# Latent attention of the prompt with its keys in the partitions, and a join without it

## Reference

```python
k_nope = einsum('bsc,chd->bshd', c_kv, w_uk);  v = einsum('bsc,chd->bshd', c_kv, w_uv)
s = (einsum(q_nope, k_nope) + einsum(q_pe, k_pe)) * MLA_SCALE    # 64 + 32 rows; MLA_SCALE = 96 ** -0.5
s = where(kpos <= qpos, s, -inf);  p = softmax(s);  ob = einsum('bhqk,bkhd->bqhd', p, v)
oa = merge of three dilated window attentions, weighted by their softmax denominators
pa = (oa * silu(za)) @ w_proj_a;   pb = (ob * silu(zb)) @ w_proj_b
```

## Time and profile before

| | |
|---|---|
| median of 3 runs | 4224.75 us (4222.05 to 4228.91) |
| the profiled execution | 4216.9 us, its span 4215.3 us |
| PE, DVE, ACT, POOL busy in it | 3469.0, 1314.7, 957.4, 281.4 us |
| latent attention, from 2385 to 3147 us of the span | 762 us |
| join, from 3617 to 3787 us | 170 us |

### The profile page before, as it was taken

How to read it: one execution, slowest core, us unless ns; L and a number is a source line. 1 busy time by engine, 2 the same in 40 slices (tenths; PEclk the granted TensorE clock), 3 DMA queues, 4 the chain that set the end, 5 groups by cost and what they waited for, 6 DMA issues and landing times. The chain is left out here.

```text
span 4215.3 us, 55290 instructions
## 1 busy us (share of the span) xinstructions
PE 3469.0 (82%) x19384; PEld 2980.1 (71%) x19384; DVE 1314.7 (31%) x3532; ACT 957.4 (23%) x1846; POOL 281.4 (7%) x308
## 2 busy tenths in 40 slices
PE   3899999999988897999999799999982444318989
PEld 3777777877776686999999677777762444318877
DVE  4122211222222122221111255555541222583333
ACT  4322211222211112222222144444430000001021
POOL 0000000000000000000000000000001222003300
PEclk6999999999978887999999899999995555559999
DMA  3233333333122223322222200000005554565443
GB/s 109 63 101 107 108 105 111 113 105 105 57 80 80 88 75 89 94 84 80 78 86 77 66 12 12 12 12 12 12 17 190 187 188 150 185 213 202 153 135 117
DMA packets 349533, 407.90 MB, mean 97 GB/s; under 512 B 113066, under 2 KB 306315, under 8 KB 347099
## 3 DMA queue, kind: packets, MB, share of 16 engines
q1 hardware_dynamic: 328330, 258.31, 20.7%
q0 software_dynamic: 21008, 147.09, 9.6%
HBM read 318.18 MB, written 175.19 MB: 117 GB/s over the span
## 5 line engine op out<-in xcount | busy, mean ns | idle before, releaser
L109 PE MATMUL dil_S<-all_xT_hi,dil_w_hi 128*128 128x512 f32 x1152 | 467.7, 406 | 17.6 <-DVE dil_w_lo L621 17.6
L110 PE MATMUL dil_S<-all_xT_lo,dil_w_hi 128*128 128x512 f32 x1152 | 461.2, 400 | 0.0
L111 PE MATMUL dil_S<-all_xT_hi,dil_w_lo 128*128 128x512 f32 x1152 | 460.3, 400 | 0.0
L109 PE MATMUL gate_ps<-all_xT_hi,gate_w_hi 128*128 128x416 f32 x960 | 346.4, 361 | 13.7 <-DVE gate_w_lo L1074 13.7
L111 PE MATMUL gate_ps<-all_xT_hi,gate_w_lo 128*128 128x416 f32 x960 | 338.1, 352 | 0.0
L110 PE MATMUL gate_ps<-all_xT_lo,gate_w_hi 128*128 128x416 f32 x960 | 337.4, 351 | 0.0
L1525 PE MATMUL mla_S<-mla_k,mla_q 96*128 96x512 f32 (+3 forms) x640 | 276.7, 549 | 15.2 <-ACT mla_p L1416 9.2
L109 PEld LDWEIGHTS dil_S<-all_xT_hi,dil_w_hi 128*128 128x128 f32 x1152 | 222.0, 193 | 67.3 <-DVE dil_w_lo L621 17.8
L1553 PE MATMUL mla_O<-mla_v,mla_pT 128*128 128x66 f32 x2176 | 264.3, 271 | 2.6 <-DVE mla_pT L1474 1.7
L1553 PEld LDWEIGHTS mla_O<-mla_v,mla_pT 128*128 128x128 f32 x2176 | 257.6, 192 | 5.0 <-DVE mla_pT L1474 2.6
L111 PEld LDWEIGHTS dil_S<-all_xT_hi,dil_w_lo 128*128 128x128 f32 x1152 | 220.5, 191 | 51.5
(11 more groups left out here) (263 smaller groups left out, 5790.0 us busy)
## 6 DMA issues: line engine op xcount, KB each, us to landing
out_win_sample<-in_state_win POOLq DMA_DIRECT2D x16, 4088.0 KB, 14.8
sdil_kv<-in_state_win SPq DMA_DIRECT2D x72, 512.0 KB
scr_gates<-gate_out POOLq DMA_DIRECT2D x120, 208.0 KB, 2.2
sdil_qb<-scr_hs SPq DMA_DIRECT2D x32, 768.0 KB
dil_raw<-in_w_in SPq DMA_DIRECT2D x36, 512.0 KB, 4.1
proj_gm<-scr_gates SPq DMA_DIRECT2D x40, 416.0 KB, 3.3
gate_ckv<-in_cache_ckv SPq DMA_DIRECT2D x256, 64.0 KB, 1.8
out_win_sample<-in_state_win POOLq DMA_DIRECT2D x4, 4064.0 KB, 2.3
```

Source lines behind the costliest of these rows:

```text
L109: pe.matmul(out, w[0], x[0], start=first, stop=False)
L110: pe.matmul(out, w[0], x[1], start=False, stop=False)
L111: return pe.matmul(out, w[1], x[0], start=False, stop=last)
```

## Change

The latent attention is written anew. A unit is now one head with 512 queries (`qb`, 4 of them); its tiles are 128 keys in the partitions by 512 queries, `4 * qb + 4` of them, of which the last four lie on the diagonal and have 512, 384, 256 and 128 queries. That is 40 tiles and 17,408 columns a head. The values of all heads are projected once, ahead (16 products of 512 columns). Queries and keys are split into high and low parts. A tile goes: scores by `split_matmul` (item A), copy to SBUF by ACT into one of 22 slots `sc`, on the diagonal the mask by DVE, running maximum over the unit's tiles by DVE; the unit's maxima are turned by PE (M1), reduced and widened by DVE, turned again (M2) and copied by ACT into `mb`, one maximum for each query in all partitions; POOL subtracts `mb` from each tile in SBUF, ACT takes the exponential in place, and PE multiplies values (64 columns beside 64 columns of ones) with the tile, so that outputs and sums come out turned (item B). DVE inverts 64x512 sums, POOL multiplies with the gates, DVE multiplies with the output, and SP stores 64x512 straight into `scr_uT`. The order of all this is a list that `latent_order` makes ahead of time. The join keeps only the dilated part.

```diff
 def stage_latent_attn(nc, t, ident):
-        RING = 6
-        S = m.ps("S", [P, 4, 512])
-        T = m.ps("T", [P, 2, 4, P])
+        RING = 22
+        LAG = 12
+        LEAD = 4
+        tiles, first, order = latent_order(RING, LAG)
+        sc = m.sb("sc", [P, RING, 512])
+        PJ = m.ps("PJ", [P, 512])
+        S = m.ps("S", [P, 2, 512])
+        T = m.ps("T", [P, 4, P])
...
+        def values_due(p, lead, begun):
+            i = begun
+            while i < NTILES and place[("B", i)] <= p + lead and place[("M2", unit(i))] <= p:
+                i += 1
+            return range(begun, i)
...
+                    sp.dma_start(causal[:, :], t["causal"].rearrange("a b -> b a")).then_inc(loaded, 16)
...
             def _(pool):
+                def weigh(n, begun):
+                    r = out_rows(n // 4)
+                    pool.wait_ge(centred, begun)
+                    pool.wait_ge(inverted, n + 1)
+                    pool.wait_ge(gz_in[n % 2], 16 * (n // 2 + 1))
...
+                    pool.tensor_tensor(rg[r, :], rv[r, :], gz[n % 2][r, :], ALU.mult).then_inc(rg_ready, 1)
...
+                    for i in values_due(p, LEAD + 3, begun):
+                        x = sc[:, i % RING, c0:512]
+                        pool.wait_ge(mb_out, n + 1)
+                        pool.tensor_tensor(x, x, mb[n % 2][:, c0:512], ALU.subtract).then_inc(centred, 1)
...
+                        act.wait_ge(s_ready, i + 1)
...
+                        act.activation(sc[:, i % RING, c0:512], S[:, i % 2, c0:512], ACT.Copy).then_inc(copied, 1)
...
+                    for i in values_due(p, LEAD, begun):
+                        act.wait_ge(centred, i + 1)
+                        act.activation(x, x, ACT.Exp, scale=B_SCALE).then_inc(exped, 1)
...
+                        dve.tensor_tensor(top[:, c0:512], old[:, c0:512], new[:, c0:512], ALU.max).then_inc(maxed, 1)
...
+                        dve.reciprocal(rv[out_rows(n // 4), :], O[s, n % 2, :]).then_inc(inverted, 1)
...
+                pe.wait_ge(loaded, 16 * 7)
...
+                        split_matmul(pe, S[:, i % 2, c0:512], [k[x][0:W, kt * P:(kt + 1) * P] for x in range(2)],
+                                     [q[x][0:W, qb * 512 + c0:(qb + 1) * 512] for x in range(2)], True, True)\
+                            .then_inc(s_ready, 1)
...
+                        pe.matmul(O[:, n % 2, c0:512], w, sc[:, i % RING, c0:512], start=kt == 0,
+                                  stop=kt == 4 * qb + 3).then_inc(pv_ready, 1)
 def stage_join(nc, t, ident, wraw):
-                    sp.dma_start(ob[b][:, 0:chunks, :, :], t["ob"][rows, 0:chunks]).then_inc(oin[b], 16)
...
-                    sp.dma_start(gz[b][:, :, :], t["gates"][0:8, :, rows].rearrange("k p n -> p k n"))\
+                    sp.dma_start(gz[b][:, :, :], t["gates"][0:4, :, rows].rearrange("k p n -> p k n"))\
...
+def latent_order(ring, lag):
...
+        if can_value() and (not can_go() or (not took_value and scored - valued > lag)):
+            order.append(("B", valued))
+            now += max((512 - tiles[valued][3]) * 0.00168, 0.23)
...
+        elif can_go():
+            item = ahead.pop(0)
+            order.append(item)
+            if item[0] == "A":
+                h, qb, kt, c0 = tiles[item[1]]
+                now += max((512 - c0) * 0.00133, 0.33)
```

More of the change, by code:

```diff
@@ new lines, in _ @@
+                for c in range(QL // P):
+                    sp.dma_start(cqT[:, c, :], t["cqT"][c, :, 0:SEQ]).then_inc(loaded, 16)
+                sp.dma_start(kpe[NOPE:W, :], t["kpeT"][:, 0:SEQ]).then_inc(loaded, 16)
+                sp.dma_start(rope[NOPE:P, :], t["rope_cols"][:, 0:SEQ]).then_inc(loaded, 16)
+                with nc.allow_non_contiguous_dma(reason="the mask, turned"):
+                    sp.dma_start(causal[:, :], t["causal"].rearrange("a b -> b a")).then_inc(loaded, 16)
@@ new lines, in _ @@
+                load_weights(1)
+                for n in range(4 * H):
+                    h, qb, b = n // 4, n % 4, n % 2
+                    if n > 1:
+                        sp.wait_ge(rg_ready, n - 1)
+                    r = out_rows(h)
+                    sp.dma_start(gz[b][r, :], t["gates"][4 + h // 2, r, qb * 512:(qb + 1) * 512]).then_inc(gz_in[b], 16)
+                    if n:
+                        store(n - 1)
+                    if qb == 2 and h < H - 2:
+                        load_weights(h + 2)
@@ L1432, in _ @@
-                each_head(act, body)
+                r, pe = slice(0, NOPE), slice(NOPE, W)
+                act.wait_ge(loaded, 16 * 7)
+                act.activation(k[0][pe, :], kpe[pe, :], ACT.Copy).then_inc(kpe_hi, 1)
+                for j in range(0, NT, 2):
+                    act.wait_ge(v_ready, j + 1)
+                    act.activation(v[:, j, :, 0:3:2, :], S[:, 0, :].rearrange("p (a s d) -> p a s d", s=2, d=HD), ACT.Copy)\
+                        .then_inc(v_out_a, 1)
+                begun = 0
@@ new lines, in body @@
+                    maxima = [rec[:, g, :, 2 * HD + 2:REC] for g in range(NG)]
+                    w3 = [heads(wt[:, g * H:(g + 1) * H]) for g in range(NG)]
+                    s3 = [heads(sl[:, g * H:(g + 1) * H]) for g in range(NG)]
+                    top = heads(mx[:, :])
+                    then(dve.tensor_tensor(top, maxima[0], maxima[1], ALU.max))
+                    then(dve.tensor_tensor(top, top, maxima[2], ALU.max))
+                    for g in range(NG):
+                        last = dve.tensor_tensor(w3[g], maxima[g], top, ALU.subtract)
@@ new lines, in body @@
+                    last.then_inc(expin, 1)
+                    dve.wait_ge(exped, i + 1)
+                    for g in range(NG):
+                        last = dve.tensor_tensor(s3[g], w3[g], sums_of[g], ALU.mult)
+                    then(last)
+                    then(dve.tensor_reduce(sums[:, :], sl[:, :].rearrange("p (g h) -> p h g", h=H), AX.X, ALU.add))
+                    then(dve.reciprocal(sums[:, :], sums[:, :]))
+                    for g in range(NG):
+                        last = dve.tensor_tensor(w3[g], w3[g], heads(sums[:, :]), ALU.mult)
```

675 lines of the change are left out of this document (383 added, 292 removed).

## The result

The changed kernel takes 4257.63 us, median of 4 runs (4254.95 to 4261.43), beside 4223.40 (4216.95 to 4228.91) for the kernel before on the same chip: a ratio of 1.0082, 95% interval 1.0065 to 1.0100. It is slower by 34 us; forecast was 4151, and the range ended at 4255. The later runs were made on several chips; each is set beside the kernel before on its own chip. The profiled execution has a span of 4253.4 us against 4215.3.

A forecast was written before the change was run, and what follows sets the result against it. PE was taken to bound latent attention, with DVE drawing level after the change, and DVE steps over loads the join. Latent attention -32 and join -42 give -74 from 4224.75: 4151 us, range 4050 to 4255.

The forecast's parts named there:

- the reciprocal: DVE, latent attention: 512 columns taken as 3.5 us, between 0.7 and 4.5; four a head are 14 us.
- PE's work: Latent attention: PE's products and turns sum to 68.7 us a head, against 92.9 before.
- the 18 us of values ahead: Start of latent attention: 16 value products, 14.8 us, plus 3 for PE's slow starting clock.
- The join: Join stage: 6.7 us a tile, 117 us in all instead of 158.8, so -42.
- The second SBUF operand: Latent attention: POOL's hold blocks DVE operations with two SBUF operands; POOL 43 us and DVE about 30 a head.
- the head's 82 us: Latent attention: 76 us from DVE with its waits for POOL, plus 6 at unit borders; bounds 69 and 112.
- Start and drain: Latent attention outside the heads: 18 us values ahead, 5 first keys and queries, 8 pipeline drain.
- the mask's load: Start of latent attention: turned mask, 16,384 four-byte pieces at 22 ns each, delays PE by 24 us; bounds 0 and 45.
- If they fall as chance has it: Latent attention: POOL's holds spread evenly over DVE's work, adding 7 to 12 us of waits to DVE's 68.6 a head.
- The borders: Unit ends in latent attention: exponentials wait for POOL's first subtraction, PE behind them; four times 1.5, 6 us a head.
- rival 5: Gaps keep PE at half clock in latent attention: some 137 us a head, 4591; sign a clock below 0.9; chance 0.03.
- Rival 4: Latent attention: DVE blocked before nearly every maximum, delaying PE; 98 a head, 4279; sign maxima above 1.2 us; chance 0.15.

The follow-up runs named there:

- the two filler runs: Filler PE products ahead of waits: in the changed kernel, head 95.9 beside 95.8; in the version with mask on PE, maximum in PSUM, later gate product, 4211 us.

## Why the prediction was wrong

**Right.** The prices of single operations: 1.55 us for a tile on PE, the reciprocal 3.35 us where 3.5 was taken from rows of 1 and 8 columns, PE's work 70.9 a head (68.7), the 18 us of values ahead (18.2). The join: 6.65 for its last tiles (6.7), -46 (-42). The second SBUF operand as what lets POOL block DVE.

**The step that failed** is the head's 82 us, by 14.7, or 118 us in eight heads. Start and drain are 13 us longer than taken, the mask's load 15 shorter, the join 3: together 113, which is the miss against the profile (+38 instead of -74). That start, drain and mask nearly cancel is luck. By its own terms:

- *"If they fall as chance has it"*, 7 to 12 us of waits of DVE for POOL, of which 7.4 were counted. Measured: DVE busy 84.2 against 65.4 of unblocked work, 18.8 us. The holds don't fall by chance, which would be 0.60 under every kind of work. DVE's work that needs no shared way (the reciprocal, much of the query's) stands at the borders, where POOL waits for that very reciprocal; POOL subtracts while DVE takes maxima, 0.77 of their time. This is +11.4. (In the working, "31 us lie under DVE's other work, 12 are waited" doesn't follow: 43 x 37 / 45 is 35, and 8 are waited, near the 7.4 that were counted. And 49.7 less 44 times 0.17 is 42.2, not 43.)
- *The borders*, 6 us, priced as POOL's delay of the exponentials. In DVE's sum their place is taken by 9.3 us of idle time beyond its gaps: +3.3. The wait itself was the wrong one: PE waits 3.7 us a head for exponentials and 14.2 for DVE, at the borders behind DVE's serial work, 8.6 us with the reciprocal in front of the widened maxima. The run without inversion shows 8.7 of the reciprocals' 10.7 us on the path.

These two terms are DVE's time, added up; they aren't yet what it would save to be rid of them. Of the 18.8 us of blocking only a part is shown to be on the path: 4.7 us a head for the maxima, none for the masks, 7.9 with POOL's subtractions gone, their own time and delay among them. How the rest divides between the order of the queues and the amount of work no run shows.

**The smaller terms.** The mask's turned load cost 9.3 us, not 24. The 22 ns a piece came from records of hundreds of bytes; in the trace the four-byte pieces take 16 ns each, 16 us on 16 engines, and the load lands 19.7 us after its issue, in rows 10.4, so that part of it was hidden. Of the clock, rival 5 asked only whether it stays at half; it fell 29 times, for 3 to 10 us each. That took 7.8 us a head of PE's time, but in the two filler runs taking more than half of it away gained nothing and 0.7. The stage's clock of 0.89 was under the sign set for rival 5, without its mechanism.

**Rival 4** said 98 a head and gave its place as DVE, blocked before nearly every maximum and late for M1 and the splits. The size (96.7) and both waits are there. Its sign, maxima above 1.2 us, didn't come (1.16). Its mechanism is half of it: taking the maxima's blocking away brings 91.1, and taking POOL's subtractions away 87.9, not 82. What the miss comes from besides is the reciprocal in a fixed queue, which the prediction counted as load and not as delay.

**Still open:** how the 91.1 divide, since re-placing work moved waits rather than removed them, and why the mask in PSUM costs 1.3 a head. An order made for these prices, with the reciprocal behind the keys' low part in all units and POOL's queue to match, wasn't tried.

## What to carry to other kernels

When two engines exclude each other, don't average their shares: ask which of their operations stand side by side in the order, and what one engine does while the other's harmless work runs. A long instruction in an in-order queue costs by what stands behind it; find the instruction at a unit's border that another engine waits for, and count everything ahead of it. A term whose waits can be moved but whose sum stays is bound by work: take the work out once to see it, before tuning places.

## What the runs showed of the hardware

- A DVE instruction with both inputs in SBUF is blocked by a POOL operation (512 columns: 1.16 us, and 0.69 without POOL's subtractions); with one input in PSUM it isn't (0.70 with POOL busy in 0.77 of its time).
- A reciprocal on DVE takes 6.5 ns a column (64x512 in 3.35 us); four of 128 take 0.93 each, 0.38 us more in all.
- A load of 16,384 pieces of four bytes, 16 ns each, delayed the start by 9.3 us against the same load in rows of 512 bytes.
- In a wait of 4.64 us PE's granted clock fell to 0.50; it stayed there for the last 1.4 us before 2896 and for some 5.5 us behind it, with PE at work, and was 1.00 again from 2902.
